# Output stages of two feed-forward layers: six seven-product blocks a half instead of four, with raw slots of their own

## The reference, cut to what matters

```python
gate, up = jnp.split(h @ w_ffn_in[l], 2, axis=-1)
x = x + rms_norm((jax.nn.silu(gate) * up) @ w_ffn_out[l], ffn_post_g[l])   # first layer

z = h @ w_in
a, b = z[..., :D_FF], z[..., D_FF:]
return (jax.nn.silu(a) * b) @ w_out                                        # second layer
```

## Time and profile before

| | |
|---|---|
| median of 3 runs | 2390.25 us (2389.15 to 2392.04) |
| the profiled execution | 2391.39 us |
| its span | 2389.4 us |
| granted TensorE clock over the span | 0.999 |
| TensorE busy | 2369.1 us (99%) |
| VectorE busy | 1848.3 us (77%) |
| ScalarE busy | 1398.8 us (59%) |
| GpSimd busy | 195.2 us (8%) |
| weight loads of the two output stages | 88 of 512 KB each a stage |

### The profile page before, as it was taken

How to read it: one execution, slowest core, us unless ns; L and a number is a source line. 1 busy time by engine, 2 the same in 40 slices (tenths; PEclk the granted TensorE clock), 3 DMA queues, 4 the chain that set the end, 5 groups by cost and what they waited for, 6 DMA issues and landing times.

```text
span 2389.4 us, 34793 instructions
## 1 busy us (share of the span) xinstructions
PE 2369.1 (99%) x12027; PEld 1977.8 (83%) x12027; DVE 1848.3 (77%) x2570; ACT 1398.8 (59%) x1939; POOL 195.2 (8%) x252
## 2 busy tenths in 40 slices
PE   9999999999999999999999999999999999999998
PEld 7888888887888888888887888998888888888887
...
GB/s 233 244 217 177 165 152 165 167 186 176 273 205 248 207 230 227 222 199 208 196 212 196 219 231 168 126 140 133 241 229 243 212 246 207 234 176 242 217 179 176
DMA packets 249217, 485.23 MB, mean 203 GB/s; under 512 B 19770, under 2 KB 22074, under 8 KB 248592
## 3 DMA queue, kind: packets, MB, share of 16 engines
...
q10 hardware_dynamic: 576, 1.05, 0.1%
...
## 4 chain that ended last, share of the span: by engine, by line
PE 94%; DVE 3%; DMA 2%; ACT 1%; issue 1%; SPq 0%; ACTq 0%; DVEq 0%
PE g L1466 10%; PE g L1467 10%; PE g L1468 10%; PE g L362 6%; PE g L364 6%; PE g L363 6%; PE g L1973 4%; PE g L1975 4%; PE g L1974 4%; PE m L1294 3%; PE m L1295 3%; PE m L1293 3%; PE g L1294 2%; PE g L1295 2%; PE g L1293 2%; DMA raw<-in_w_ffn_out 1%
## 5 line engine op out<-in xcount | busy, mean ns | idle before, releaser
L350 DVE TENSOR_TENSOR wl<-raw,wh 128x1024 fp32r<-128x1024 f32 (+1 forms) x500 | 601.0, 1216 | 328.5 <-ACT wh L346 321.7
L346 ACT ACTIVATE wh<-raw 128x1024 fp32r<-128x1024 f32 (+1 forms) x499 | 519.1, 1052 | 468.1 <-PE g L364 128.8
L1466 PE MATMUL g<-wh,act_hi 128*128 128x512 f32 x640 | 250.5, 391 | 0.0
L1468 PE MATMUL g<-wh,act_lo 128*128 128x512 f32 x640 | 249.3, 390 | 0.0
L1467 PE MATMUL g<-wl,act_hi 128*128 128x512 f32 x640 | 249.3, 389 | 0.0
L1232 ACT ACTIVATE wh<-in_x 128x1024 fp32r<-128x1024 f32 (+1 forms) x160 | 152.7, 955 | 106.6 <-PE g L1468 69.5
L1466 PE MATMUL g<-wh,ht_hi 128*128 128x512 f32 x544 | 212.1, 390 | 0.3 <-DVE wl L350 0.3
L1467 PE MATMUL g<-wl,ht_hi 128*128 128x512 f32 x544 | 211.8, 389 | 0.0
L1468 PE MATMUL g<-wh,ht_lo 128*128 128x512 f32 x544 | 211.8, 389 | 0.0
L1394 DVE TENSOR_TENSOR wl<-raw,wh 128x1024 fp32r<-128x1024 f32 x160 | 195.5, 1222 | 13.1 <-ACT wh L1389 3.4
L362 PE MATMUL g<-wh,act_hi 128*128 128x512 f32 x512 | 203.3, 397 | 0.9 <-DVE wl L350 0.4
...
## 6 DMA issues: line engine op xcount, KB each, us to landing
raw<-in_w_in SPq DMA_DIRECT2D x111, 512.0 KB, 4.5
raw<-in_w_ffn_in SPq DMA_DIRECT2D x106, 512.0 KB, 4.8
raw<-in_ffn_w_in SPq DMA_DIRECT2D x106, 512.0 KB, 4.8
raw<-in_w_ffn_out SPq DMA_DIRECT2D x88, 512.0 KB, 5.3
raw<-in_ffn_w_out SPq DMA_DIRECT2D x88, 512.0 KB, 5.2
raw<-in_nsa_w_in SPq DMA_DIRECT2D x80, 512.0 KB, 4.3
raw<-in_w_out SPq DMA_DIRECT2D x32, 512.0 KB, 4.3
raw<-in_nsa_w_out SPq DMA_DIRECT2D x32, 512.0 KB, 4.9
```

The lines of the kernel that those rows point to most:

```text
L346: nc.scalar.activation(wh[:, j % SLOTS, 0:n], raw[:, j % SLOTS, 0:n], ACT.Copy).then_inc(hi_done, 1)
L350: nc.vector.tensor_tensor(wl[:, j % SLOTS, 0:n], raw[:, j % SLOTS, 0:n], wh[:, j % SLOTS, 0:n].bitcast(F32), ALU.subtract).then_inc(lo_don ...
L1466: nc.tensor.matmul(dst, h, whk, start=(t in starts and k == 0), stop=False)
L1468: ins = nc.tensor.matmul(dst, l, whk, start=False, stop=(last and k == 1))
```

## The change

`FO_K` goes from 4 to 6. The order has 112 positions, sevens at 9, 16, 23, 30, 37, 44 in the first half and 64, 71, 78, 85, 92, 99 in the second, three units between neighbours. A stage has 64 units and 12 sevens where it had 72 and 8. Each seven takes its weights from memory of its own (`fo_slots`: a slot for "up", one for t3 and t1, one for t2 and t4, in space that `x`, or the gains of the end, hold at other times) and from `fifth`; units alone use the four raw slots. The sums are four 512-wide additions spread over the block: t3 and t1 ahead of q0's conversion, t2 behind it, t4 behind q1's. Rows' sums stand behind positions 3, 13 and 27, their low parts four positions further and in two operations of 256 and 768 columns, since one of the four sums now goes into free columns of `ht_hi` and `ht_lo`. SP issues the next block's two loads five positions behind a block's q0, after a wait for that block's t4. The rows `x` come, in `fo1`, after the last block has used its slots, in a burst of eight; in `fo2` six early and two behind the last block, and behind them the gain that stands in `g_a`.

```diff
-FO_K = 4
-FO_GAPS = ((10, 0), (5, 0), (1, 4), (1, 6), (1, 8)), ((6, 0), (6, 0), (4, 3), (1, 6), (1, 9))
-FO_SUMS_AT = (6, 15)
+FO_K = 6
+FO_GAPS = (((9, 0), (3, 0), (3, 0), (0, 3), (0, 3), (0, 3), (1, 7)),
+           ((8, 0), (3, 0), (3, 0), (1, 2), (0, 3), (0, 3), (1, 8)))
+FO_SUMS_AT = (3, 13, 27)
...
+OUT_UNIT_AT = [n for n, o in enumerate(OUT) if o[0] == "unit"]
...
-        fo_hi = at("fo_hi", [P, FO_K, 4, P], o_ah, F32R)
-        fo_lo = at("fo_lo", [P, FO_K, 4, P], o_ah + 8192, F32R)
...
+        fo_slots = {"fo1": [in_x[:, k] for k in range(3)],
+                    "fo2": [at("in_gb", [P, 2, NB], o_gb + 4096)[:, :, :], in_g[:, 0:2, :], in_g[:, 2:4, :]]}
...
-        def sp_behind(sp, cyc, j, src):
...
-        def act_seven(act, cyc, j, q, landed):
-        def dve_weight_sums(dve, cyc, j, landed, t2_made):
...
+        def act_seven(act, name, c, b, n, q):
...
+                act.wait_ge(ff_step, fo_t_no(name, c, b, "t1" if q == 2 else "t4"))
+            act.wait_ge(unit_used, u0 + n + 1)
+            nc.scalar.activation(quarter_of(wh, n, q), fo_source(name, q), ACT.Copy).then_inc(hi_done, 1)
...
+        def act_out_unit(act, name, n):
+            s, r = gemms[name], OUT_UNIT_AT.index(n)
+            act.wait_ge(raw_full[r % SLOTS], fo_raw_no(s, r))
+            act.wait_ge(unit_used, s["u0"] + n + 1)
+            nc.scalar.activation(wh[:, n % SLOTS, :], raw[:, r % SLOTS, :], ACT.Copy).then_inc(hi_done, 1)
+
+        def dve_out_unit(dve, name, n):
+            s, r = gemms[name], OUT_UNIT_AT.index(n)
+            dve.wait_ge(hi_done, s["u0"] + n + 1)
+            nc.vector.tensor_tensor(wl[:, n % SLOTS, :], raw[:, r % SLOTS, :], wh[:, n % SLOTS, :].bitcast(F32), ALU.subtract)\
+              .then_inc(lo_done, 1)
+
+        def dve_weight_sum(dve, name, c, b, key):
+            up, t31, t24 = fo_slots[name]
+            k = FO_K * c + b
+            behind = OUT_AT[k - 1] + (3 if key == "t1" else 4) if k else 0
+            dve.wait_ge(lo_done, SLOTS + gemms[name]["u0"] + behind)
+            if key == "t1":
+                dve.wait_ge(ahead_in, fo_ahead_no(name, FO_K * c + b))
+                dve.wait_ge(up_in, fo_up_no(name, FO_K * c + b))
+                nc.vector.tensor_tensor(t31[:, 0, :], up[:, 0, :], up[:, 1, :], ALU.add)
+                nc.vector.tensor_tensor(t31[:, 1, :], up[:, 0, :], fifth[:, 0, :], ALU.add).then_inc(ff_step, 1)
+            elif key == "t2":
+                dve.wait_ge(ff_step, fo_t_no(name, c, b, "t1"))
+                nc.vector.tensor_tensor(t24[:, 0, :], t31[:, 1, :], up[:, 1, :], ALU.add).then_inc(ff_step, 1)
+            else:
+                dve.wait_ge(ff_step, fo_t_no(name, c, b, "t2"))
+                nc.vector.tensor_tensor(t24[:, 1, :], t24[:, 0, :], fifth[:, 1, :], ALU.add).then_inc(ff_step, 1)
...
+            u0 = SLOTS + gemms[out_name]["u0"]
+            last = OUT_AT[2 * FO_K - 1]
             for n in range(8):
-                pool.wait_ge(lo_done, SLOTS + gemms[out_name]["u0"] + 4 + 2 * n)
+                if n == (0 if out_name == "fo1" else 6):
+                    pool.wait_ge(unit_used, u0 + last + 4)
+                    at_n = last + 4 - n
+                elif n == 0:
+                    at_n = 4
+                pool.wait_ge(lo_done, u0 + (at_n + n if out_name == "fo2" else last + 4 + n // 2))
...
+            def block(k):
+                c, b = OUT[OUT_AT[k]][1:3]
+                if k:
+                    sp.dma_start(fifth, columns(2 * c, b)).then_inc(ahead_in, 16)
+                sp.dma_start(fo_slots[name][0], columns(2 * c + 1, b)).then_inc(up_in, 16)
+
+            for r, n in enumerate(OUT_UNIT_AT):
+                _, c, u, _ = OUT[n]
+                if r < SLOTS:
                     sp_unit(sp, cyc, n, columns(c, u))
-                if kind == "seven" and q == 1:
-                    sp_unit(sp, cyc, n, columns(2 * c + 1, u))
-                    sp_behind(sp, cyc, n + 3, columns(*OUT[n + 3][1:3]))
-                if n + 1 in OUT_AT:
-                    sp.dma_start(raw[:, SLOTS, :].rearrange("p (k n) -> p k n", k=2), columns(2 * OUT[n + 1][1], OUT[n + 1][2]))\
-                      .then_inc(ahead_in, 16)
+                else:
+                    sp.wait_ge(lo_done, SLOTS + s["u0"] + OUT_UNIT_AT[r - SLOTS] + 1)
+                    if r < 2 * SLOTS:
+                        sp.sem_inc(raw_full[r % SLOTS], 4 * (len(OUT) - len(OUT_UNIT_AT)))
+                    sp.dma_start(raw[:, r % SLOTS, :].rearrange("p (k n) -> p k n", k=2), columns(c, u)).then_inc(raw_full[r % SLOTS], 16)
+                if r == SLOTS - 1:
+                    sp.dma_start(fifth, columns(0, 0)).then_inc(ahead_in, 16)
+                if r == 2 * SLOTS - 2:
+                    sp.wait_ge(ff_step, ff_stepped({"fo1": "ff1", "fo2": "ff2"}[name], PAIRS, 1))
+                    block(0)
+                for k in range(2 * FO_K - 1):
+                    if n == OUT_AT[k] + 5:
+                        sp.wait_ge(lo_done, SLOTS + s["u0"] + OUT_AT[k] + 2)
+                        sp.wait_ge(ff_step, fo_t_no(name, *OUT[OUT_AT[k]][1:3], "t4"))
+                        block(k + 1)
...
+                    if kind == "seven":
+                        act_seven(act, name, c, u, n, q)
                     else:
-                        act_unit(act, cyc, n)
+                        act_out_unit(act, name, n)
...
-                if n - 2 in FO_SUMS_AT:
-                    b = FO_SUMS_AT.index(n - 2) + 1
-                    act_sums_hi(act, fo_sums[:, :, :, :], fo_hi[:, 2 * (b - 1):2 * b, :, :], summed_no(name, b) + 1)
+                if n - 4 in FO_SUMS_AT:
+                    r = FO_SUMS_AT.index(n - 4)
+                    act.wait_ge(ff_summed, summed_no(name, r + 1) + 1)
+                    nc.scalar.activation(first_sums(ht_hi, 4 * r), fo_sums[:, :, 0, :], ACT.Copy)
+                    act_sums_hi(act, fo_sums[:, :, 1:4, :], fo_hi[r][:, :, :, :], summed_no(name, r + 1) + 1)
...
+                for k, key in enumerate(("t1", "t2", "t4")):
+                    if n + 1 - k in OUT_AT:
+                        dve_weight_sum(dve, name, *OUT[n + 1 - k][1:3], key)
                 if n in FO_SUMS_AT:
                     dve_sums_of_x(dve, ht_hi, ht_lo, 4 * FO_SUMS_AT.index(n), fo_whole, fo_sums)
-                if n - 2 in FO_SUMS_AT:
-                    b = FO_SUMS_AT.index(n - 2) + 1
-                    k = slice(2 * (b - 1), 2 * b)
-                    dve_sums_lo(dve, fo_sums[:, :, :, :], fo_hi[:, k, :, :], fo_lo[:, k, :, :], summed_no(name, b) + 1)
-                    dve.wait_ge(ff_summed, summed_no(name, b + 1))
-                if n == OUT_AT[FO_K - 1] + 7:
+                if n - 4 in FO_SUMS_AT:
+                    r = FO_SUMS_AT.index(n - 4)
+                    dve.wait_ge(ff_summed, summed_no(name, r + 1) + 2)
+                    nc.vector.tensor_tensor(first_sums(ht_lo, 4 * r), fo_sums[:, :, 0, :], first_sums(ht_hi, 4 * r).bitcast(F32), ALU.subtract)
+                    dve_sums_lo(dve, fo_sums[:, :, 1:4, :], fo_hi[r][:, :, :, :], fo_lo[name][r][:, :, :, :], summed_no(name, r + 1) + 1)
+                    dve.wait_ge(ff_summed, summed_no(name, r + 2))
+                if name == "fo2" and n == OUT_AT[FO_K - 1] + 7:
+                    dve.wait_ge(x_moved, x_moved_no("ff2", 2) - 32)
+                if n == (len(OUT) - 1 if name == "fo1" else OUT_AT[2 * FO_K - 1] + 10):
```

More of the change, by code:

```diff
@@ L168, in build @@
         fo_sums = at("fo_sums", [P, 2, 4, P], o_al + 4096)
-        fo_hi = at("fo_hi", [P, FO_K, 4, P], o_ah, F32R)
-        fo_lo = at("fo_lo", [P, FO_K, 4, P], o_ah + 8192, F32R)
+        fo_hi = [at(f"fo_hi{r}", [P, 2, 3, P], o_ah + (0, 3072, 12288)[r], F32R) for r in range(FO_K // 2)]
+        fo_lo01 = [at(f"fo_lo{r}", [P, 2, 3, P], o_ah + 6144 + 3072 * r, F32R) for r in range(2)]
+        fo_lo = {"fo1": fo_lo01 + [at("fo_lo2", [P, 2, 3, P], o_x + 12288, F32R)],
+                 "fo2": fo_lo01 + [at("fo_lo3", [P, T, D], o_x, F32R)[:, :, 3 * NB:3 * NB + 3 * P].rearrange("p t (k n) -> p t k n", k=3)]}
+        in_g = at("in_g", [P, 6, NB], o_ga)
+        fo_slots = {"fo1": [in_x[:, k] for k in range(3)],
+                    "fo2": [at("in_gb", [P, 2, NB], o_gb + 4096)[:, :, :], in_g[:, 0:2, :], in_g[:, 2:4, :]]}
         fo_kept = {"fo1": at("fo_kept1", [P, T, NB], o_ga + 4096), "fo2": at("fo_kept2", [P, T, NB], o_gb)}
@@ L1063, in build @@
         LAYER = {"ff1": 0, "ff2": 1, "fo1": 0, "fo2": 1}
-        FO_STEPS = 2 * (FO_K + 6)
-        FO_STEP = {"t2": 1, "u2": FO_K + 1, "u3": FO_K + 2, "gate": FO_K + 3, "up": FO_K + 4, "rest": FO_K + 5}
+        FO_STEPS = 2 * (3 * FO_K + 6)
+        FO_STEP = {"t1": 1, "t2": 2, "t4": 3} | {key: 3 * FO_K + n + 1 for n, key in enumerate(("u2", "u3", "gate", "up", "rest"))}
         T2_STEPS = [1 + 2 * b + (at > MUL_AT) for b, at in enumerate(SUM_AFTER)]
@@ L1116, in ff_used, with fo_t_no @@
             return SLOTS + s["u0"] + FF_FIRST - FF_NEXT + FF_NEXT * i + j + 1
```

(26 more changed lines are left out.)

30 lines of the change are left out of this document (15 added, 15 removed).

## The result

The changed kernel takes 2396.07 us (median of 13 runs, 2393.71 to 2397.76) against 2390.51 (13 runs of before beside them): ratio 1.0021, 95% interval 1.0013 to 1.0029. It is slower by 5.6 us where 1.1 less was forecast; the time lies inside the stated range (2384.5 to 2398), near its upper end.

A forecast was written before the change was run, and what follows sets the result against it. TensorE's matmul count times spacing, plus its waits, was taken as the bound. Matmuls -5.4, old stalls -1.3, new stalls +5.6 gave -1.1 us, so 2389.1 us; range 2384.5 to 2398.

The forecast's parts named there:

- The saving: TensorE, both output stages: 24 matmuls fewer at 0.2267 us spacing, 5.4 us saved.
- VectorE's stalls in the first half: TensorE waiting for late conversions in each output stage's first half: 2.8 us a stage, 5.6 in two.
- the late unit: Unit at positions 14 and 28, behind the rows' sums, reaches TensorE late: stall 0.59 + 0.1 each.
- every q2 behind the low parts: q2's conversion late at TensorE: 0.26 + 0.1 in block 1, 0.76 + 0.1 in block 3.
- The 0.76 forecast for block 3: Stall ahead of block 3's q2: t4 at +0.19 plus low parts 1.33 and 1.28, 2.80 against 2.04 wanted.
- The load loop: From t4 through three loads and conversions to next t4: 13.69 us against TensorE's 12.92, each block 0.77 later.
- I take 7.1: SyncE's queue: third load lands 7.1 us after t4, between 6.9 at best and 8.2 at worst.
- the second rival: Third load at 7.5 us, lag grows 1.17 a block, stalls 16.8 us, time 2400; decides from about 7.2; chance 0.20.
- the limit of +0.76: Latest end of t4 against its block's first matmul, in us, before TensorE waits for q2.
- The rule that spoke against it: Skill's DMA formula for block loads: three after 5.6 us, loop closes in 12.4; set aside for slower trace rows.
- Costed at nothing: the x rows.: First stage's burst of eight x loads behind the last block: wanted some 19 us on, loads at most 12.0.
- the rivals: Includes the burst: first stage's last raws land after 12 us, TensorE waits about 2, time 2391; chance 0.05.

The follow-up runs named there:

- the split: Changed kernel with next block's loads and low parts one unit later, x burst behind last weight load, and rows' sums in two pieces: 2385.34 us, ratio 0.9976.
- the first experiment: Changed kernel with the next block's two loads issued one unit later, behind the load of the last unit before that block: 2391.42 us, ratio 1.0003.

## Why the prediction was wrong

- **The saving.** 24 matmuls went, at 0.2267 us each. Right.
- **VectorE's stalls in the first half.** Places and sum (5.7 for 5.6) as forecast; the late unit 0.60 to 0.77 for 0.69, and the split, where nothing else held the blocks back, took all four away. But part of the sum was right by chance: with unit first (the first experiment) every q2 behind the low parts is late by 0.12 + 0.11, where block 1 had 0.26 + 0.1, and block 5 is not late at all. The 0.76 forecast for block 3 had the lag of the loads in it. What blocks 3 and 5 lost beyond the 0.12 (the longest was 1.18) was the loads' part, unevenly spread.
- **The load loop.** The step that failed is "I take 7.1" in "What it adds on the queues". The mechanism was right and its size off: from t4's end the third load took 7.35 by the median of 22, and 7.58 in the turn shown, for 7.1; a turn took 13.85 in the mean of the second stage's second half, and 14.07 in the turn shown, for 13.69. The text itself named about 7.2 as the point where the second rival, "the loads set the pace", decides; I gave it 0.20. At 0.92 a block t4 reaches -3.2 + 5 x 0.92 = +1.4, past the limit of +0.76, and the second halves stall. Cost 3.5 us in the second halves, and 4.6 us in all by the first experiment. In the first stage two turns were slower still: the second load of the pair landed 6.5 and 5.8 us after its issue where it otherwise took 5.0 to 5.3. What was in its way the trace does not say; this stays open.
- **The rule that spoke against it.** The Trainium skill (DMA: Bandwidth & Descriptors, Anatomy of one DMA) gives 2.0 us and bytes over 436 GB/s, a fit for transfers that GpSimd issues; SyncE issues these. By the estimate that the prediction made of it, three loads are there after 5.6 us and the loop closes in time (with the prediction's own terms in 12.2 us, not 12.4). Here the trace disagrees: the first of the three took 3.8 us, the second 5.3 and the third 6.6 from their issues, so the third was there 7.5 us after the first issue.
- **"Costed at nothing: the x rows."** The second failed step. The cover I named (the rows are wanted 19 us later) protects x, not the weight loads that were on their way beside it; those took up to 12.9 us and TensorE waited 1.96. In the rivals I had the size right (2) and the chance too low. Moving the burst gave 2.3 us.
- **The gain and pieces of x at the end of the second stage** were not costed: 0.83 us. `g_a` was moved only where 0.20 of it was left, so the cause there is not settled.
- **The range** held because the second rival's 2400 had been taken in, and that is partly luck, for the 2400 counts time twice. Its sum lets the lag of the loads grow through the first half and adds VectorE's stalls on top, while the forecast, rightly, takes each stall off the lag. By the forecast's own steps a growth of 1.17 gives 0.69 + 0.36 + 0.69 + 1.66 + 1.01 = 4.4 in a first half for 6.3, with 2.1 in a second half 13.0 for 16.8, and a time of 2396.6. The measured 2396.07 lies near that, but is made up otherwise: 3.0 of its 12.2 us stand at the ends of the stages.
